# The lo parts of 55 weight tiles of the second mixing: subtracted by GpSimd instead of VectorE

## What is computed

```python
proj = h @ w_in[l]
q_lat, kv_lat, k_pe, gq, gk, gv, ga, gb, gz, gates = jnp.split(proj, split_at, axis=-1)
...
qkv = jax.nn.silu(causal_depthwise_conv(qkv, w_conv))
q = l2norm(to_chunks(q, DK)) * (DK ** -0.5)
k = l2norm(to_chunks(k, DK))
...
T = lax.linalg.triangular_solve(A + eye, eye, left_side=True, lower=True, unit_diagonal=True)
w = jnp.einsum('bhnij,bhnjd->bhnid', T, k_beta * jnp.exp(decay)[..., None])
u = jnp.einsum('bhnij,bhnje->bhnie', T, v * beta[..., None])
```

## Time and profile before

| | us |
|---|---|
| median of 3 runs | 3398.58 (3393.21 to 3403.74) |
| the profiled execution | 3402.77 |
| its span, first to last instruction | 3401.0 |
| TensorE busy in the span | 3249.2 |
| VectorE busy | 2045.5 |
| ScalarE busy | 1330.5 |
| GpSimd busy | 593.9 |
| mean granted TensorE clock, share of full | 0.973 |

### The profile page before, as it was taken

The page is one execution under the profiler, slowest core; times in us unless marked ns, Lnnn a source line. Parts: engine busy times, 40 slices in busy tenths (PEclk is TensorE's granted clock), DMA queues, the critical chain, the costliest instruction groups (busy, mean ns, idle before and its releaser), DMA issues.

```text
span 3401.0 us, 40709 instructions
## 1 busy us (share of the span) xinstructions
PE 3249.2 (96%) x16107; PEld 2690.4 (79%) x16107; DVE 2045.5 (60%) x3541; ACT 1330.5 (39%) x2339; POOL 593.9 (17%) x573
## 2 busy tenths in 40 slices
PE   8999999999999999999799998899998999989998
PEld 5764899998888888888688885788787667778887
DVE  5766887876888888888655436445543345443333
ACT  3131238883444444444322225454443124233322
POOL 0001349971222222221000000000000000000000
PEclk9999999999999999999899998999998999989999
DMA  7426244569999999997255422121221122222322
GB/s 258 131 79 230 75 139 160 208 236 343 336 326 334 337 327 331 337 332 278 90 184 185 160 79 89 59 90 63 75 85 58 39 86 76 93 81 94 99 93 80
DMA packets 190206, 574.40 MB, mean 169 GB/s; under 512 B 16576, under 2 KB 82112, under 8 KB 171712
## 3 DMA queue, kind: packets, MB, share of 16 engines
q1 hardware_dynamic: 152144, 367.96, 31.6%
q0 software_dynamic: 37872, 203.84, 16.6%
HBM read 523.89 MB, written 47.84 MB: 168 GB/s over the span
## 4 chain that ended last, share of the span: by engine, by line
PE 82%; DVE 7%; ACT 4%; DMA 3%; POOL 2%; issue 1%; SPq 0%; DVEq 0%; ACTq 0%; POOLq 0%
PE ps L237 11%; PE ps L238 11%; PE ps L239 11%; PE ps L1627 5%; PE ps L1628 5%; PE ps L1626 5%; PE ps L1382 4%; PE ps L1384 4%; PE ps L1383 4%; PE ps L602 2%; PE ps L246 2%; DMA hidden_dram<-peerg_HS 2%; PE ps L171 1%; DMA adaw_AW<-w_ada 1%; PE ps L605 1%; PE ps L2289 1%
## 5 line engine op out<-in xcount | busy, mean ns | idle before, releaser
L229 DVE TENSOR_TENSOR Wl<-W,Wh 128x1024 fp32r<-128x1024 f32 (+2 forms) x337 | 407.6, 1210 | 694.5 <-ACT Wh L217 694.4
L217 ACT ACTIVATE Wh<-W 128x1024 fp32r<-128x1024 f32 x363 | 377.5, 1040 | 553.5 <-PE ps L239 519.2
L1382 PE MATMUL ps<-peer_Hh,Wh 128*128 128x384 f32 x1024 | 348.3, 340 | 2.7 <-DVE Wl L229 1.9
L1384 PE MATMUL ps<-peer_Hh,Wl 128*128 128x384 f32 x1024 | 344.5, 336 | 0.0
L1383 PE MATMUL ps<-peer_Hl,Wh 128*128 128x384 f32 x1024 | 344.0, 336 | 0.0
L1595 POOL DMA_INDIRECT peerv_UV<-peer_uv,peer_EX x128 | 209.3, 1635 | 639.4 <-DVE peer_Y L1663 583.9
L1626 PE MATMUL ps<-peerv_VH,peer_HTh 128*128 128x512 f32 x768 | 299.0, 389 | 2.5 <-DVE peer_HTl L1689 2.5
L1628 PE MATMUL ps<-peerv_VH,peer_HTl 128*128 128x512 f32 x768 | 300.5, 391 | 0.0
L1627 PE MATMUL ps<-peerv_VL,peer_HTh 128*128 128x512 f32 x768 | 300.2, 391 | 0.0
L237 PE MATMUL ps<-f_Hh,Wh 128*128 128x512 f32 x672 | 262.3, 390 | 2.2 <-DVE Wl L229 2.2
L239 PE MATMUL ps<-f_Hh,Wl 128*128 128x512 f32 x672 | 261.5, 389 | 0.0
(11 more groups left out here) (497 smaller groups left out, 6530.2 us busy)
## 6 DMA issues: line engine op xcount, KB each, us to landing
W<-peer_u SPq DMA_DIRECT2D x128, 512.0 KB, 6.9
peerv_VR<-peer_v SPq DMA_DIRECT2D x128, 512.0 KB, 5.3
gates_dram<-peerg_GB SPq DMA_DIRECT2D x12, 2048.0 KB, 7.3
peerv_GR<-gates_dram SPq DMA_DIRECT2D x32, 768.0 KB, 8.3
f_AW<-w_ada POOLq DMA_DIRECT2D x48, 512.0 KB, 4.3
W<-w_gate SPq DMA_DIRECT2D x44, 512.0 KB, 3.2
W<-w_up SPq DMA_DIRECT2D x44, 512.0 KB, 3.3
swa_AW<-w_ada POOLq DMA_DIRECT2D x32, 512.0 KB, 4.3
```

Of the source, the lines that this page charges most:

```text
L217: A.then_inc(e.activation(w_parts(i)[0], w_raw(i), ACT.Copy), ("w_hi", i))
L229: (G if i in lo_on_pool else V).then_inc(e.tensor_tensor(lo, w_raw(i), hi.bitcast(F32), SUB), ("w", i))
L1382: e.matmul(o, hi[:, k, :], H2[0][:, k, 0:TD], start=k == 0, stop=False)
L1384: ins = e.matmul(o, lo[:, k, :], H2[0][:, k, 0:TD], start=False, stop=k == 7)
```

## The change

```diff
     def rows_dve(e):
         for n in range(NROW + 2):
-            if 0 < n < NROW - 1:
-                w_lo(e, t_row[n + 1])
             if n == 1:
                 decay_dve(e)
...
+    lo_on_pool.update(t_row[2:])
+
     def rows_pool(e):
-        for s, key in enumerate(spill):
-            A.wait_ge(e, ("row_out", at_row[key]))
-            spl_out[s % NSP].then_inc(e.dma_start(LD[s], SPL[:, s % NSP, :]), ("spl", s))
+        for n in range(NROW):
+            if 0 < n < NROW - 1:
+                w_lo(e, t_row[n + 1])
+            if ROWS[n] in spill:
+                s = spill[ROWS[n]]
+                A.wait_ge(e, ("row_out", n))
+                spl_out[s % NSP].then_inc(e.dma_start(LD[s], SPL[:, s % NSP, :]), ("spl", s))
```

## The result

The kernel after takes 3408.66 us, the median of ten executions (3403.63 to 3410.33). Beside them on the same chip the kernel before took 3401.16. The ratio is 1.0022, with a 95% interval of 1.0013 to 1.0031: 7.5 us slower. That is less than the 0.3% (10.2 us) which the prediction took for what a measurement can tell, but the interval leaves out 1. The profiled execution took 3410.33, its span is 3408.5 against 3401.0 before, with the same mean clock of 0.973. So one profile of each shows a difference of the same size.

A forecast was written before the change was run, and what follows sets the result against it. The prediction took TensorE to bound the stage. Longer waits 6.6, engines holding each other up 2.1 and norms 1.0 made 9.7 us, added to the median 3398.58 for 3408.3 us; range 3400 to 3414.

The forecast's parts named there:

- The size of the lag: From hi to a row's first matmul: 2.51 us with GpSimd against 1.40 with VectorE, so lo is 1.11 us later.
- Term 1, the longer wait: TensorE waits longer for lo at rows 24, 40, 56, 37, 53, 27, 13 and row 3: 6.6 us.
- rows 2 and 3 at +0.5: Start of the stage: both rows wait, but the decays' copy starts earlier; 0.5 us taken of a possible 0.1 to 1.2.
- Term 2, the engines hold each other up: Head starts at rows 9 and 25: GpSimd's subtraction and VectorE's L2366 take shared ports in turn, 2 x 1.03 = 2.1 us.
- Term 3, the norms: VectorE's L2154, run 16 times, ends 0.5 us late beside GpSimd; between 0 and 8.0 us, taken as 1.0.
- Only the wait is longer: Rival: the ports don't meet as the pair overlaps less; 6.6 us slower, 3405.2 us; chance 0.18.
- The ports meet everywhere: Rival: L2154 passes on 0.5 us each of 16 times; 16.7 us slower, 3415 us; chance 0.12.
- 16 meetings: In the norms, each of L2154's 16 calls was called certain to meet GpSimd's subtraction, 0.5 us each.
- Covered: Rival: TensorE's queue swallows the lag as VectorE and ScalarE run ahead; 3399 to 3402 us; chance 0.15.
- Faster by 15 us: Rival: unblocked VectorE brings L2362 and L2373 forward at head starts; 21.6 us won, 6.6 lost, 3383.6 us; chance 0.05.
- a stage shorter than before: Sign: under 512 us from row 0 to row 56 would show the reading of who waits for whom wrong.

The follow-up runs named there:

- lo last: Against the kernel after, TensorE does the 16 matmuls needing only hi first, then waits for lo; all lo of rows 2 to 56 on GpSimd: 3398.71 us, ratio 0.999.

## Why the prediction was right, and what it missed

The forecast was 3408.3 us in a range of 3400 to 3414; measured were 3408.66. That it is met within 0.4 us is luck. The forecast stands on 3398.58, the median of three runs, and the kernel before takes 3401.16 in the median of ten, 2.6 us more; the loss is 7.5 us where the sum had 9.7, 2.2 less. The two errors cancel. The mechanisms were right, and the parts of the sum compare so: rows 0 to 11, +1.5 forecast (0.5 and 1.03) and -0.99 measured; rows 11 to 56, 8.2 forecast (6.14, 1.03 and 1.0) and 8.69 measured.

**The size of the lag** was put at 1.11 us. It measured 1.17 at row 24, and rows 40 and 56 gave +1.17 and +1.16. GpSimd's instruction was right (2.39 us); the rest is in the hand-overs.

**Term 1, the longer wait**, held. Rows 24, 40 and 56: 3.50 us for 3.33. Row 37 +1.0 and row 53 +1.0 for 0.92 each, row 27 +0.76 for 0.70, row 13 +0.34 for 0.27: 6.6 in all for 6.14, and the larger lag explains the difference. Putting these seven rows back removed their steps, and so did the other order of passes. TensorE's wait for the lo was forecast at some 10 us and is 9.9, but 2.5 of them are in rows 2 and 4. One sentence of the term was wrong by its own numbers, "the other rows have over a microsecond spare": a row needs 1.11 + 0.14 = 1.25 us between lo and matmul to lose nothing, and rows 15, 28 and 29 had 1.12, 1.02 and 1.09, so 0.88 to 0.98 to spare.

**The step that failed** is the last of term 1, rows 2 and 3 at +0.5. Row 2 is late by 1.16, but by row 6 the kernel is 2.14 ahead. Rows 0 to 11 are 2.5 us better than forecast, rows 11 to 56 0.5 worse: the difference between 9.7 and 7.7. The text had seen that the copy for the decays no longer stands behind row 2's lo, and priced it only as a smaller loss, 0.5 of a possible 0.1 to 1.2. It did not follow what the copy starts, and it did not ask what clock TensorE would have in the rows behind. What the traces show is a copy 5.22 us earlier, a lost gap of 1.17 us ahead of row 3, and slow stretches of the clock in other rows. How the 2 us divide between these was not settled, as the first ten rows of the same kernel differ by 2 us between executions.

**Term 2, the engines hold each other up**, held in place and size: 0.99 and 0.95 us at rows 9 and 25 for 1.03 each. L2366 took 1.69 at the place of the earlier trace rows (forecast: about 1.7), and it fell back to 0.69 when one subtraction was moved. The prediction looked at these two places alone. Five of the eight heads' L2366 are held, 7.9 us of VectorE in total, of which TensorE sees 1.9.

**Term 3, the norms**, was taken at 1.0 between 0 and 8.0. L2154 went to 1.02 us in the mean (forecast 1.1), 5.2 us in the sum; it was held in 12 of 16 calls, eleven times by 0.47. Small steps of 0.24 us stand at rows 15, 29, 32 and 46, 1.0 together, so the number is met. But half of it is not this term. Rows 15 and 29 were 0.20 and 0.23 us short of the measured lag already (1.12 and 1.09 between lo and matmul, 1.17 + 0.15 needed). Rows 32 and 46 were not (1.40 and 1.39), so there the hi must have come later too, and that this is the held norms is argued, not isolated by a run. With lo last all four steps are gone while L2154 stays at 1.03 us, so the delay did reach TensorE through the wait for the lo, as the term said.

**The rivals.** Only the wait is longer (6.6): contradicted by row 25. The ports meet everywhere (16.7): they don't, the "16 meetings" that it called certain were 12, and of these only the steps at rows 32 and 46 can have reached TensorE. Covered: the seven rows contradict it. Faster by 15 us: TensorE's wait for L2362 stayed at 12.2 for 12.1; VectorE's idle time moved to its waits for TensorE and ScalarE. The prediction had one of its tests badly put: that a stage shorter than before would show a wrong reading of the waits. The first rows were shorter and the reading of rows 11 to 56 was right.

## What to carry to other kernels

Work that an idle engine could do costs what its result comes later to the one who waits, not what it takes off the engine that does it now. Count the rows in which the result has less spare time than the new lag, and price only those: here seven of 55 rows made 6.6 of the 8.7 us from row 11 on. Before moving such work, look whether the consumer can ask for it later; 16 matmuls that don't need the lo, put ahead of the 8 that do, gave back what the choice of engine had cost (from +8.69 to +0.10 over rows 11 to 56).

## What the runs showed of the hardware

- The same fp32 subtraction of 128x1024 takes 1.225 us on VectorE and 2.39 us on GpSimd, a fill of that size on GpSimd 0.95 us.
- The start of the stage does not repeat: rows 0 to 11 of an unchanged kernel lasted 2.08 us longer in a second execution, rows 11 to 56 only 0.08. In these first rows the granted clock changes between 0.50 and 1.00 from one slice of 5 us to the next, and which rows fall into the slow part decides microseconds. Later it does so in single rows: the same 24 matmuls of row 42 took 7.30 us at 0.77 and 5.71 at 1.00. A profile of one execution can't price a change there.
- A held instruction shows in a profile as a longer one: L2366 is recorded from its issue, 1.69 us, and nothing under waits names GpSimd. It is found by the mean of its group (1673 for 692 ns) and by its end: for all 19 held instructions it lies 0.55 or 0.56 us behind that of GpSimd's subtraction. A GpSimd fill, which only writes, held up none of the three L2366 that it met.
